# A two-block transformer forward pass on one core: two PSUM banks for late transposes, a regrouped token gather, and no idle TensorE products around the routing

## The reference

```python
h = jnp.einsum('bsd,dc->bsc', x, w_in[l])
o_a = sliding_window_sink_attn(...)      # 8 heads
o_b = indexer_sparse_attn(...)           # 4 heads
o_c = mla_attn(...)                      # 4 heads
mix = jnp.concatenate([o_a, o_b, o_c], axis=-1)
x = layer_norm(DEEPNORM_ALPHA * x + jnp.einsum('bsm,md->bsd', mix, w_out[l]), ln1_g[l], ln1_b[l])
x = layer_norm(DEEPNORM_ALPHA * x + moe_ffn(x, w_router, router_bias, w_gate[l], w_up[l], w_down[l]), ln2_g[l], ln2_b[l])
```

```python
scores = jax.nn.sigmoid(jnp.dot(xt, w_router))
group_score = jnp.sum(lax.top_k(biased, TOP_K)[0], axis=-1)
g_sel = jnp.argmax(group_score, axis=-1)
h = jax.nn.silu(jnp.einsum('nd,edf->enf', xt, w_gate)) * jnp.einsum('nd,edf->enf', xt, w_up)
y = jnp.einsum('enf,efd->nd', h * gates.T[:, :, None], w_down)
```

## Time and profile before

| what | value |
|---|---|
| median of three runs | 1079.59 us (1078.99 to 1079.83) |
| profiled execution, its own time | 1079.66 us |
| its span from first to last instruction | 1077.9 us |
| PE busy | 1049.3 us, 97% of the span |
| DVE busy | 722.9 us, 67% |
| ACT busy | 554.1 us, 51% |
| chain that ended last: PE, DVE, ACT, POOL | 84%, 7%, 3%, 3% |

### The profile page before, as it was taken

One profiled execution on the slowest core, in us unless ns is written; L12 is line 12 of the kernel. 1 busy time (PEld: TensorE's weight loads), 2 busy tenths in 40 slices (PEclk: granted clock), 3 DMA queues, 4 the chain that ended last, 5 costly groups with the idle time before them and its releaser, 6 DMA issues.

```text
span 1077.9 us, 15208 instructions
## 1 busy us (share of the span) xinstructions
PE 1049.3 (97%) x5742; PEld 858.8 (80%) x5742; DVE 722.9 (67%) x1032; ACT 554.1 (51%) x766; POOL 90.6 (8%) x141
## 2 busy tenths in 40 slices
PE   9999999999999999999999999999999999999997
PEld 8899987888888888888887766777788877667765
DVE  5533634488787667678777745786788778357856
ACT  5444455682643444456763534665367635346741
POOL 3000020100000000004600000000028000000000
PEclk9999999999999999999999999999999999999998
DMA  9773344445465655544221888997353118789971
GB/s 292 224 224 119 117 150 156 157 157 188 133 228 193 195 195 192 175 135 136 106 101 40 331 279 332 375 324 259 105 181 119 64 55 300 259 325 373 346 273 39
DMA packets 108016, 214.20 MB, mean 199 GB/s; under 512 B 7602, under 2 KB 52298, under 8 KB 107952
## 3 DMA queue, kind: packets, MB, share of 16 engines
q1 hardware_dynamic: 105072, 209.38, 56.5%
q0 software_dynamic: 1312, 3.88, 1.1%
q10 hardware_dynamic: 1568, 0.10, 0.1%
HBM read 212.24 MB, written 1.09 MB: 198 GB/s over the span
## 4 chain that ended last, share of the span: by engine, by line
PE 84%; DVE 7%; ACT 3%; POOL 3%; issue 1%; DMA 1%; SPq 0%; DVEq 0%; ACTq 0%; POOLq 0%
PE ps L977 18%; PE ps L979 18%; PE ps L978 18%; PE ps L1130 7%; PE ps L1129 3%; PE ps L1102 2%; PE ps L1712 2%; PE ps L1068 2%; PE ps L1734 1%; PE ps L1087 1%; ACT whi L1847 1%; POOL arena L921 1%; PE ps L1393 1%; PE ps L1420 1%; PE ps L1060 1%
## 5 line engine op out<-in xcount | busy, mean ns | idle before, releaser
L2311 DVE TENSOR_TENSOR wlo<-raw,whi 128x2048 fp32r<-128x2048 f32 (+4 forms) x143 | 311.6, 2181 | 157.7 <-ACT whi L1847 157.0
L1847 ACT ACTIVATE whi<-raw 128x2048 fp32r<-128x2048 f32 (+4 forms) x145 | 261.6, 1808 | 162.8 <-PE ps L979 70.3
L977 PE MATMUL ps<-whi,act_both 128*128 128x512 f32 (+2 forms) x440 | 165.3, 376 | 0.3 <-DVE wlo L2311 0.3
L979 PE MATMUL ps<-whi,act_both 128*128 128x512 f32 (+2 forms) x440 | 161.0, 366 | 0.0
L978 PE MATMUL ps<-wlo,act_both 128*128 128x512 f32 (+2 forms) x440 | 160.9, 366 | 0.0
L977 PE MATMUL ps<-whi,mix_hi 128*128 128x512 f32 x332 | 130.5, 393 | 1.4 <-DVE mix_lo L2871 0.5
L979 PE MATMUL ps<-whi,mix_lo 128*128 128x512 f32 x332 | 129.2, 389 | 0.0
L978 PE MATMUL ps<-wlo,mix_hi 128*128 128x512 f32 x332 | 129.1, 389 | 0.0
L1130 PE MATMUL ps<-act_both,whi 128*128 128x512 f32 x336 | 116.4, 396 | 0.0
L2311 DVE TENSOR_TENSOR wlo<-arena,whi 128x2048 fp32r<-128x2048 f32 (+1 forms) x36 | 76.0, 2113 | 37.8 <-ACT whi L1847 37.7
L977 PEld LDWEIGHTS ps<-whi,act_both 128*128 128x128 f32 x440 | 82.9, 188 | 19.4 <-issue 6.1
(11 more groups left out here) (351 smaller groups left out, 1724.8 us busy)
## 6 DMA issues: line engine op xcount, KB each, us to landing
raw<-in_w_in SPq DMA_DIRECT2D x43, 1024.0 KB, 5.3
raw<-in_w_down SPq DMA_DIRECT2D x23, 1024.0 KB, 6.1
raw<-in_w_gu SPq DMA_DIRECT2D x22, 1024.0 KB, 5.1
raw<-in_w_out SPq DMA_DIRECT2D x12, 1024.0 KB, 5.1
raw<-in_w_gate SPq DMA_DIRECT2D x24, 512.0 KB, 5.7
raw<-in_w_up SPq DMA_DIRECT2D x24, 512.0 KB, 6.8
arena<-in_w_gate SPq DMA_DIRECT2D x20, 512.0 KB, 5.1
arena<-in_w_up SPq DMA_DIRECT2D x20, 512.0 KB, 6.4
```

The source lines that it names most:

```text
L977: pe.matmul(o, ah, bh, start=first, stop=False)
L979: return pe.matmul(o, al, bh, start=False, stop=last)
L1847: act.activation(whi[:, c % 3, 0:n], raw_of(c, v)[:, 0:n], ACT.Copy).then_inc(hi_made, 1)
L2311: dve.tensor_tensor(wlo[:, c % 3, 0:n], raw_of(c, v)[:, 0:n], whi[:, c % 3, 0:n].bitcast(F32), ALU.subtract)\
```

## The change

Four things are edited, in both layers of the second block.

In the unit loop the transposes of units 8 and 10 go to bank 3 instead of bank 2, and from unit 8 on `turn_probs` waits for the copy of the unit before the last one instead of the last one. `MIX_BANK` and `OUT_BANK` get other banks to fit. `out_part(0, 0)` waits for one of the two remainders of the first half of the mix; the wait for the second stands behind it now.

The gather is regrouped: the products with the rounded tokens of four chunks come first, and then the four chunks' products with the remainders, so the first product waits for the rounded tokens and `put` alone.

On VectorE the second piece of `rest_of` moves from before the ranks to behind `put`.

All 24 idle products of a layer are taken out. Those at the start of the program, behind its first transposes, and at the start of the second layer stay.

```diff
-MIX_BANK = ((3, 4), (5, 3))
-OUT_BANK = (0, 6)
+MIX_BANK = ((5, 4), (2, 3))
+OUT_BANK = (0, 4)
...
-WARM = {1: 1, 12: 1}
...
-            return dict(t=t, w=w, n=len(heads), flipped=t == 1, joint=False, par=i % 2, slot=i % 4, probs=i % 3 * 512, one_bank=True, kind=kind, pairs=(j0, j0 + two),
+            return dict(t=t, w=w, n=len(heads), flipped=t == 1, joint=False, par=i % 2, slot=i % 4, turn_bank=3 if i in (8, 10) else 2, apart=i >= 8, probs=i % 3 * 512, one_bank=True, kind=kind, pairs=(j0, j0 + two),
...
-                    pe.wait_ge(pt_ready, n)
+                    pe.wait_ge(pt_ready, n - 1 if u.get("apart") else n)
...
-                o = banks(2, 4)
+                o = banks(u["turn_bank"], 4)
...
-                    if i in WARM:
-                        keep_warm(2 if i == 1 else 3, WARM[i])
...
-                        pe.wait_ge(tr_lo, l * 12 + 2)
+                        pe.wait_ge(tr_lo, l * 12 + 1)
                         out_part(0, 0)
...
+                pe.wait_ge(tr_lo, l * 12 + 2)
                 out_part(1, 0)
...
                 turn(x_tok, 0, l * 8, True)
-                keep_warm(5, 6)
...
-                keep_warm(5, 4)
                 turn(x_tok, 1, l * 8, True)
...
-                keep_warm(7, 6)
                 pe.matmul(group_key, fours, cst[:, C_G8:C_G8 + 8].rearrange("p (a g) -> p a g", a=2), start=True, stop=False)
...
-                keep_warm(7, 6)
                 pe.wait_ge(put_ready, l + 1)
-                pe.wait_ge(xt_l, l * 4 + 2)
+                pe.wait_ge(xt_h, l * 2 + 2)
                 n = 2 * P + 64
-                for k in range(KD):
-                    if k == KD // 2:
-                        pe.wait_ge(xt_l, l * 4 + 4)
-                    for t in range(TT):
-                        pe.matmul(ps[:, k, 0:n], xk_hi[:, t, k, :], put[:, t, 0:n], start=t == 0, stop=False)
-                        x = pe.matmul(ps[:, k, 0:n], xk_lo[:, t, k, :], put[:, t, 0:n], start=False, stop=t == TT - 1)
-                    x.then_inc(xg_full, 1)
+                for half in range(2):
+                    chunks = range(4 * half, 4 * half + 4)
+                    for k in chunks:
+                        for t in range(TT):
+                            pe.matmul(ps[:, k, 0:n], xk_hi[:, t, k, :], put[:, t, 0:n], start=t == 0, stop=False)
+                    pe.wait_ge(xt_l, l * 4 + 2 * half + 2)
+                    for k in chunks:
+                        for t in range(TT):
+                            x = pe.matmul(ps[:, k, 0:n], xk_lo[:, t, k, :], put[:, t, 0:n], start=False, stop=t == TT - 1)
+                        x.then_inc(xg_full, 1)
...
                 dve.max_index(vec8, sorted_key, key_sb).then_inc(ord_ready, 1)
-                rest_of(1, slice(0, 1))
...
                 ins.then_inc(put_ready, 1)
+                rest_of(1, slice(0, 1))
```

More of the change, by code:

```diff
@@ L626, in unit_first @@
                 w = S if t else P
-                return dict(t=t, w=w, n=3, flipped=True, low=[x % 2 for x in heads], joint=True, par=u % 2, slot=u % 4, probs=u % 2 * 768, one_bank=False, scale=SCALE,
+                return dict(t=t, w=w, n=3, flipped=True, low=[x % 2 for x in heads], joint=True, par=u % 2, slot=u % 4, turn_bank=2, probs=u % 2 * 768, one_bank=False, scale=SCALE,
                             q=[qa[64 * (x % 2):64 * (x % 2) + 64, x // 2, t * P:(t + 1) * P] for x in heads],
@@ L634, in unit_first @@
             w = S if t else P
-            return dict(t=t, w=w, n=len(heads), flipped=True, low=[x % 2 for x in heads], joint=False, par=u % 2, slot=u % 4, probs=u % 2 * 768, one_bank=False, scale=SCALE,
+            return dict(t=t, w=w, n=len(heads), flipped=True, low=[x % 2 for x in heads], joint=False, par=u % 2, slot=u % 4, turn_bank=2, probs=u % 2 * 768, one_bank=False, scale=SCALE,
                         q=[qc[64 * (x % 2):64 * (x % 2) + 64, x // 2, t * P:(t + 1) * P] for x in heads],
@@ L1877, in probs_out @@
                 m = u["n"] * u["w"]
-                act.activation(turned_at(u)[:, 0:m], banks(2, 4)[:, 0:m], ACT.Copy).then_inc(pt_ready, 1)
+                act.activation(turned_at(u)[:, 0:m], banks(u["turn_bank"], 4)[:, 0:m], ACT.Copy).then_inc(pt_ready, 1)
             act.dma_start(ident, I["shape_consts"][:, 0:P]).then_inc(c_in, 16)
```

## The result

The changed kernel takes 1082.45 us (median of 8 runs, 1081.50 to 1084.64) against 1079.41 us of the kernel before beside it: a ratio of 1.0031, 95% interval [1.0022, 1.0039], so 0.3% slower. Its profiled execution took 1082.24 us, its span 1080.4 us.

What follows compares the result with a forecast made beforehand. TensorE was taken as the bound (84% of the span on the last-ending chain). From 1079.66 us, edits gave -2.99 at full clock and clock falls +2.8 and +1.85: +1.66, so 1081.3, range 1076.6 to 1084.8.

Steps and rivals of the forecast that it cites:

- The likeliest case: Granted clock falls ahead of the routing and of the gather in each layer: 1081.3 us, own range 1078.5 to 1084.5, chance 50%.
- Two banks: Unit loop to output projection: values 0.47 us earlier, one subtraction's wait saves 0.64; 1.11 a layer, 2.22 in all.
- Idle products as PE time: All 24 idle products of a layer stand inside waits that go on; removing them at unchanged clock is worth 0.
- The gather: Gather starts 0.97 us earlier a layer; the first expert's second weight part lets only 0.06 + 0.71 = 0.77 through.
- The clock ahead of `ord_ready`: Routing products, small transposes and counting products at half clock: 1.4 us lost a layer (bounds 0 and 2.6), +2.8 in all.
- The clock at the gather: Half clock costs the gather 1.5 us a layer (bounds 0 and 2.65); after the unused lead, +0.6 and +1.25, together +1.85.
- The 5.3 us that the bounds rest on: Low clock lasts some 5 us of unbroken products, from program start: twelve idle products took 5.40 us, 3.28 at full clock.
- No fall: Rival: idle products were not needed and the clock holds; 1076.7 us, 1077.5 without the gather's gain; chance 20%.
- a fall only ahead of the gather: Rival: the routing keeps its clock and only the emptier stretch from 587.8 on drops it; 1078.5 us, chance 17%.
- A fall in the unit loop: Rival: the clock also falls where steps 1 and 12 lose idle products, up to +2.65 us a layer; 1085, chance 13%.
- The upper estimate of 1086: If transposes in the remaining stretches don't count as busy for the clock, both clock losses reach their upper bounds: about 1086 us.

Runs made afterwards that it cites:

- loop_out: The kernel before without the two idle products of each layer's unit loop, all others kept: 1080.55 us, ratio 1.0005.
- gather_only: The kernel before with only the regrouped gather and the moved piece of `rest_of`, banks and idle products as before: 1080.20 us, ratio 1.0009.
- turns_old_gather: The changed kernel with 44 idle transposes a layer in the four places, but gather and `rest_of` as before: 1077.03 us, ratio 0.9974.
- idle_back: The changed kernel with 22 idle products a layer back in four places from output projection to gather: 1077.89 us, ratio 0.9983.
- idle_turns: The changed kernel with 44 idle 128x128 transposes a layer in the four places from output projection to gather: 1077.31 us, ratio 0.9978.

## Why the prediction was right, step by step

The forecast was 1081.3, the measured time 1082.45, on the side forecast and inside the range. The rise itself was forecast at 1.66 us and measured at 3.0 (1082.45 less 1079.41). The likeliest case, a fall ahead of the routing and another ahead of the gather in each layer, is what the trace shows.

**Two banks.** Forecast -1.11 a layer, measured -1.06 in layer 0 (554.84 to 554.09, and the 0.31) and -1.04 in layer 1 (+1.61 in the unit loop, +0.57 at the output projection). The steps were right too: the values 0.5 early, the rest of the way 0.45 to 0.47, and 0.6 from waiting for one subtraction.

**Idle products as PE time.** Forecast 0; loop_out agrees within its interval for the unit loop, and the waits behind groups of six grew by 1.39 each (0.92 to 2.31, 0.68 to 2.07), where six had kept PE busy for 1.64, their drain included; ahead of the gather, where `put` came earlier too, from 1.37 to 1.82.

**The gather.** It began 0.95 earlier (594.88 to 593.93) in spite of the +0.11 ahead of it. Forecast 0.77 of 1.94 through at full clock; the times of gather_only and turns_old_gather show none of it. The trace of gather_only, of its fastest run, has both slacks as they were read (0.07 and 0.73, of the second 0.14 already at the output projection), and the lead still stands at 947.94, where the kernel before is at 948.88. So the reading of the rows held in that execution; why the median doesn't keep the gain stays open. With the banks' gain on top the weight part eats more, 0.95 and 1.01 in idle_back.

**The clock ahead of `ord_ready`.** Forecast 1.4 a layer. Measured +0.92 in layer 0 (-0.81 to +0.11) and +1.96 in layer 1 (+0.57 to +2.53), 1.44 on average. The layers differ because the clock came back in the middle of the 36 products in layer 0 (0.91 over 586 to 588) and not before their end in layer 1 (0.50 over 888 to 890 there). So the 1.4 is the mean of two unlike values from one execution.

**The clock at the gather.** Forecast, with the regrouping's 0.77, +0.5 in layer 0 and +0.55 in layer 1. Measured +1.62 (+0.11 to +1.73) and +0.94 (+2.53 to +3.47). This is the term that was sized too small: the gather of layer 0 ran 7.5 us where it took 4.8, a loss of 2.7 and thus the upper bound, where 1.5 was taken. In layer 1 the gather lost just the 1.5 (897.07 to 903.36, before 895.10 to 899.89), since the clock came back within it (0.90 over 900 to 902), but half of the lead was gone ahead of it: the four steps of counting products stood 0.43 apart instead of 0.23, and the gather came 0.55 closer to the first of them instead of 1.05 as in layer 0. The 5.3 us that the bounds rest on come from durations alone: the view of the clock shows 1.00 over 5 to 7 us, amid the twelve slow products of the earlier trace rows. About 0.9 of it was given back at 948, where a wait of 0.80 vanished, which no step of the prediction had.

**The sum.** Over both layers the traces give -2.10 for the banks, +2.88 for the routing, +2.56 for the gather with its regrouping and -0.86 at 948, where the forecast had -2.22, +2.8, +1.08 and nothing; 0.31 of the rise was there ahead of the edits. More than half of the 1.5 us that the gather was sized too small was thus made up for by a gain that nobody had foreseen. The mechanism was right; that the total came within 1.2 us is in part luck.

**The rivals.** No fall, and a fall only ahead of the gather, are refuted by the trace; the first shows in idle_back and idle_turns as 1077.9 and 1077.3, where 1076.7 was forecast (1077.5 without the gather's gain). A fall in the unit loop didn't come. The upper estimate of 1086, in which transposes are no cover, was not needed for this result, and idle_turns speaks against its ground.

The best version of the study keeps the two banks and puts idle transposes into the four waits: 1077.0 to 1077.3, 0.22% to 0.26% under the kernel before.

## What to carry to other kernels

Work that nobody reads, in a wait that goes on behind it, costs nothing by the timeline and can still be worth its place: here 22 such products a layer held the clock for the routing and the gather behind them, some 8 us over two layers, while the two in the unit loop made no difference that shows (loop_out). So ask of idle work not what wait it lies in but what dense work comes next, and read the granted clock by stretch before taking it out. A lead that ends at a weight transfer which does not move is worth only the slack of that transfer; and a delay may be given back at a wait further on.

## What was not expected of the hardware

A single wait of 2.09 us among dense products was followed by a granted clock of 0.68 over the next stretch (loop_out, 952 to 956), so there the late data cost more than the wait. And 44 idle transposes of 128x128 a layer kept the clock at 1.00 where 22 products of 512 columns did.
